# Attention scores of two maps: from zero-padded queries on all 128 rows of the array to the two halves of 64 rows

## The reference, cut to what matters

```python
logits = jnp.einsum('bqhmd,bkhmd->bhmqk', q, k).astype(jnp.float32) * (DA_DH ** -0.5)   # m: the two maps, d: 64
logits = jnp.where((dist >= 0)[None, None, None], logits + bias[None, :, None], -1e30)
p = jax.nn.softmax(logits, axis=-1)
attn = p[:, :, 0] - lam * p[:, :, 1]
return jnp.einsum('bhqk,bkhv->bqhv', attn, v.astype(jnp.float32))
```

## Time and profile before

| | |
|---|---|
| median of 3 runs | 1911.32 us (1902.96 to 1913.05) |
| the profiled execution's own time | 1919.13 us |
| its span, first to last instruction | 1917.2 us |
| PE busy over the span | 1675.8 us (87%) |
| DVE, ACT, POOL busy | 714.6, 454.0, 255.2 us |
| mean granted PE clock, share of full | 0.932 |
| the attention phase on PE | from 486 us (bias) or 491 us (first z) to 911.5 us |

### The profile page before, as it was taken

How to read it: one execution, slowest core, us unless ns; L and a number is a source line. 1 busy time by engine, 2 the same in 40 slices (tenths; PEclk the granted TensorE clock), 3 DMA queues, 4 the chain that set the end, 5 groups by cost and what they waited for, 6 DMA issues and landing times. The chain is left out here.

```text
span 1917.2 us, 22028 instructions
## 1 busy us (share of the span) xinstructions
PE 1675.8 (87%) x7437; PEld 1114.3 (58%) x7438; DVE 714.6 (37%) x1501; ACT 454.0 (24%) x1062; POOL 255.2 (13%) x447
## 2 busy tenths in 40 slices
PE   5998889975898989897789699999989946999996
PEld 4565555655455655565344588888867833444443
DVE  4367676676244444534122321111132241222111
ACT  2233333232243333333121311011032210111110
POOL 1000101010221222221313000000000001222221
PEclk8999899987898989998899799999989967999998
DMA  7001200000302020000866211121043364988873
GB/s 219 1 1 56 67 1 24 1 24 2 95 1 57 1 58 0 25 1 24 272 214 217 80 34 34 34 65 34 1 125 103 124 208 144 303 246 238 244 214 62
DMA packets 135895, 175.00 MB, mean 91 GB/s; under 512 B 9523, under 2 KB 106854, under 8 KB 135798
## 3 DMA queue, kind: packets, MB, share of 16 engines
q1 hardware_dynamic: 123190, 129.71, 21.4%
q0 software_dynamic: 12608, 44.05, 8.5%
HBM read 142.86 MB, written 30.87 MB: 91 GB/s over the span
## 5 line engine op out<-in xcount | busy, mean ns | idle before, releaser
L941 PE MATMUL psum<-branch_part,kept 128*128 128x384 f32 (+1 forms) x576 | 205.6, 514 | 1.2 <-DVE branch_part L1171 1.2
L2164 PE MATMUL psum<-moe_part,kept 128*128 x416 | 185.6, 599 | 5.9 <-issue 4.3
L941 PEld LDWEIGHTS psum<-branch_part,kept 128*128 128x128 f32 (+1 forms) x576 | 110.7, 197 | 78.6 <-issue 22.2
L475 PE MATMUL psum<-kept,branch_part 128*128 128x368 f32 x384 | 125.2, 482 | 10.0 <-PEq L218 5.0
L1598 PE MATMUL psum<-kept,merge_part 128*128 128x368 f32 x384 | 125.2, 480 | 9.5 <-DMA merge_part<-w_da_out 9.5
L1604 PE MATMUL psum<-split 128*128 128x368 f32 x384 | 133.4, 347 | 0.0
L2164 PEld LDWEIGHTS psum<-moe_part,kept 128*128 128x128 f32 x416 | 77.6, 192 | 95.4 <-issue 94.8
L480 PE MATMUL psum<-branch_part,kept 128*128 128x512 f32 (+1 forms) x288 | 127.6, 598 | 1.3 <-DVE kept L661 1.3
L1605 PE MATMUL psum<-split 128*128 128x368 f32 x384 | 126.9, 330 | 0.0
L1606 PE MATMUL psum<-split 128*128 128x368 f32 x384 | 126.5, 329 | 0.0
L1653 DVE TENSOR_TENSOR merge_part<-merge_part,psum 128x368 f32<-128x368 f32 x48 | 23.6, 534 | 253.6 <-ACT merge_part L1629 253.6
(11 more groups left out here) (321 smaller groups left out, 2701.9 us busy)
## 6 DMA issues: line engine op xcount, KB each, us to landing
branch_part<-cache_k SPq DMA_DIRECT2D x64, 256.0 KB, 4.8
branch_part<-cache_v POOLq DMA_DIRECT2D x64, 256.0 KB, 5.1
moe_part<-w_gate SPq DMA_DIRECT2D x16, 1024.0 KB, 7.0
moe_part<-w_up SPq DMA_DIRECT2D x16, 1024.0 KB, 13.2
moe_part<-w_down SPq DMA_DIRECT2D x16, 1024.0 KB, 14.0
branch_part<-w_in SPq DMA_DIRECT2D x8, 1024.0 KB, 8.8
merge_part<-w_in SPq DMA_DIRECT2D x16, 512.0 KB
branch_part<-w_in SPq DMA_DIRECT2D x12, 512.0 KB
```

The lines of the kernel that those rows point to most:

```text
L475: mm = pe.matmul(bank[:, 0:CH], Wb[0][:, k, c0:c0 + P], K["xT"][:, k, CH * i:CH * i + CH], start=(k == 0), stop=(k == KC - 1))
L941: mm = pe.matmul(bank_of(("z", h, i))[:ROWS[i], 0:384], K["xT"][:, k, cols(i)], Wb[h % 2][:, k, :], start=(k == 0), stop=(k == KC - 1))
L2164: mm = pe.matmul(psum[:, 2 + par, :], XT[par][:, k, :], K["GU"][:, bass.ds(KC * b + k, 1), :], start=(k == 0), stop=(k == KC - 1))
```

## The change

The two zero-padded copies `qz` become one `qT` of the same 128 rows without zeros. Scores of map 0 are a matmul on rows 0 to 63 of query and key, scores of map 1 one on rows 64 to 127. The jobs L(s,0) and L(s,1) become one job, in which each piece (up to 512 columns) is issued for map 0 and then for map 1. `place_qk` copies the queries in one instruction instead of two. The two memsets go. `save` copies each half of the rows for itself, with a drain of POOL ahead of each copy and one more. In `meta_scores` PE waits, between the maps, for its own first matmul.

```diff
-            slot += [("L", s, 0), ("L", s, 1)] + ([("e", s, 0)] if s % NQ == NQ - 1 else [])
+            slot += [("L", s, 0)] + ([("e", s, 0)] if s % NQ == NQ - 1 else [])
...
-        qz = [sb(2, TOK) for _ in range(2)]
+        qT = [sb(TOK) for _ in range(2)]
...
-            def scores(s, m):
+            def scores(s):
                 h, i = s // NQ, s % NQ
                 r = P if i else META
-                q = qz[h % 2][:, m, COL[i]:COL[i] + r]
-                if m == 0:
-                    pe.wait_ge(x_done, NT * h + i + 1)
-                    if s:
-                        pe.wait_ge(exp_done, 2 * s)
+                rows = [slice(64 * m, 64 * m + 64) for m in range(2)]
+                pe.wait_ge(x_done, NT * h + i + 1)
+                if s:
+                    pe.wait_ge(exp_done, 2 * s)
                 n = P * i
-                for c in range(0, n, 512):
-                    w = min(512, n - c)
-                    mm = pe.matmul(lg[m][:r, c:c + w], q, kT[h % 2][:, FIRST + c:FIRST + c + w], start=True, stop=True)
-                if n < SEQ:
-                    mm = pe.matmul(lg[m][:r, n:n + META], q, kT[h % 2][:, 0:META], start=True, stop=True)
-                    mm.then_inc(logits, 1)
-                elif m == 0:
-                    mm.then_inc(logits, 1)
+                pieces = [(c, min(512, n - c), FIRST + c) for c in range(0, n, 512)] + [(n, META, 0)] * (n < SEQ)
+                for at, w, key in pieces:
+                    for m in range(2):
+                        mm = pe.matmul(lg[m][:r, at:at + w], qT[h % 2][rows[m], COL[i]:COL[i] + r], kT[h % 2][rows[m], key:key + w], start=True, stop=True)
+                        if at + w >= n and (n == SEQ or at == n) and (n < SEQ or m == 0):
+                            mm.then_inc(logits, 1)
...
+                    if m == 0:
+                        mm.then_inc(meta_scored, 1)
+                        pe.wait_ge(meta_scored, h + 1)
                 mm.then_inc(logits, 1)
...
-                for m in range(2):
-                    rows = slice(64 * m, 64 * m + 64)
-                    act.activation(qz[h % 2][rows, m, cols(i)], bank[rows, 0:r], ACT.Copy, scale=K["vecT"][rows, 18:19])
+                act.activation(qT[h % 2][:, cols(i)], bank[:, 0:r], ACT.Copy, scale=K["vecT"][:, 18:19])
...
-            for h in range(2):
-                pool.memset(qz[h].rearrange("p a b -> p (a b)"), 0.0).then_inc(setup, 1)
             pool.memset(K["Qs"].rearrange("p a b -> p (a b)"), 0.0).then_inc(setup, 1)
-            pool.wait_ge(setup, 3)
+            pool.wait_ge(setup, 1)
```

More of the change, by code:

```diff
@@ L852, in phase_attention @@
         kv_out = [sem("kv_out0"), sem("kv_out1")]
+        meta_scored = sem("meta_scored")
         Wb = [sb(KC, 384) for _ in range(2)]
-        qz = [sb(2, TOK) for _ in range(2)]
+        qT = [sb(TOK) for _ in range(2)]
         kT = [sb(TOK) for _ in range(2)]
@@ L974, in meta_scores @@
                 for m in range(2):
-                    mm = pe.matmul(bank_of(("e", s, 0))[:, META * m:META * m + META], qz[h % 2][:, m, cols(i)],
-                                   kT[h % 2][:, 0:META], start=True, stop=True)
+                    rows = slice(64 * m, 64 * m + 64)
+                    mm = pe.matmul(bank_of(("e", s, 0))[:, META * m:META * m + META], qT[h % 2][rows, cols(i)],
+                                   kT[h % 2][rows, 0:META], start=True, stop=True)
+                    if m == 0:
+                        mm.then_inc(meta_scored, 1)
+                        pe.wait_ge(meta_scored, h + 1)
                 mm.then_inc(logits, 1)
@@ L1013, in _ @@
                 pe.matmul(psum[:, h, 0:ND], relh[0:33, h, :], bucket[0:33], start=True, stop=True).then_inc(bias_made, 1)
-            run = {"z": product, "x": turn_qk, "L": scores, "e": lambda s, _: meta_scores(s), "a": turn_probabilities,
+            run = {"z": product, "x": turn_qk, "L": lambda s, _: scores(s), "e": lambda s, _: meta_scores(s), "a": turn_probabilities,
                    "o": lambda s, _: outputs(s), "g": lambda s, _: turn_output(s)}
@@ L1042, in place_qk @@
                 act.wait_ge(x_turned, n + 1)
-                if n == 0:
-                    act.wait_ge(setup, 3)
                 if i == 0 and h >= 2:
                     act.wait_ge(saved, h - 1)
-                for m in range(2):
-                    rows = slice(64 * m, 64 * m + 64)
-                    act.activation(qz[h % 2][rows, m, cols(i)], bank[rows, 0:r], ACT.Copy, scale=K["vecT"][rows, 18:19])
+                act.activation(qT[h % 2][:, cols(i)], bank[:, 0:r], ACT.Copy, scale=K["vecT"][:, 18:19])
                 act.activation(kT[h % 2][:, cols(i)], bank[:, P:P + r], ACT.Copy).then_inc(x_done, 1)
@@ L1138, in save @@
                 for m in range(2):
-                    pool.tensor_copy(K["Qs"][:, DB * h:DB * h + DB, 16 * h + 8 * m:16 * h + 8 * m + 8],
-                                     qz[h % 2][:, m, META:FIRST].rearrange("p (b s) -> p b s", s=DS))
+                    rows = slice(64 * m, 64 * m + 64)
+                    pool.drain()
+                    pool.tensor_copy(K["Qs"][rows, DB * h:DB * h + DB, 16 * h + 8 * m:16 * h + 8 * m + 8],
+                                     qT[h % 2][rows, META:FIRST].rearrange("p (b s) -> p b s", s=DS))
+                pool.drain()
                 pool.tensor_copy(K["kS"][:, h, :], kT[h % 2][:, 0:FIRST]).then_inc(saved, 1)
```

## The result

The changed kernel takes 1930.22 us (median of 4 runs, 1927.18 to 1933.03). The kernel before, run beside it, takes 1909.61 us (1902.96 to 1913.05). The ratio is 1.0112, 95% interval 1.0079 to 1.0145. So the change costs about 21 us, or 1.1%. 1920 was forecast, with a range of 1905 to 1940.

What follows compares the result with a forecast made beforehand. The prediction took each attention slot to be bound by map 0's scores and DVE up to `normalise`, not by PE. Its terms, -2.0 + 3.8 - 2.0 + 8.7 = +8.5 us, gave 1920 us against 1911.32, range 1905 to 1940.

Steps and rivals of the forecast that it cites:

- The chain of the slot: Attention slot: it ends when DVE has normalised; from map 0's end to x are 4.01 us, map 1's 1.73 beside them.
- Entering the halves, +3.8: Scores in blocks 4 to 8: switching PE to 64-row halves delays map 0 by 0.19 us in 20 slots, +3.8 us.
- map 1 no longer in DVE's way, -2.0: Scores: DVE no longer waits for map 1, which ends beside map 0; 0.5 us a head, -2.0 us.
- The start, -2.0: Start of attention phase: with two memsets gone DVE's copy is quicker and bias matmuls start 2.7 us earlier; -2.0 us taken.
- The clock, +8.7: Slots of blocks 4 to 7: longer PE waits drop the clock in 5 of 16 slots, 1.73 us each, +8.7 us.
- slower: Whole kernel: time more than 0.5%, some 9.6 us, above the kernel before; chance 0.46.
- within: Whole kernel: time within 0.5%, some 9.6 us, of the kernel before, told as no change; chance 0.45.
- Rival A: PE's clock in the attention phase: waits of 1 to 2 us leave it alone, sum -0.2 us, 1911 us; chance 0.15.
- B: Scores on PE: the halves do not run together, so DVE starts later; +34.5 us, 1946 us; chance 0.17.
- C: Attention phase: PE is the bound after all, so the 31 us saved on scores come out; 1878 us; chance 0.08.

Runs made afterwards that it cites:

- the second one: Trace of the kernel before, run again with no edit, against the kernel before: 1909.69 us, ratio 1.0009.
- the last experiment: Changed kernel with `normalise` ahead of the maxima, plus four useless 512-column matmuls ahead of the outputs in each slot of block 8, against the kernel before: 1886.11 us, ratio 0.9877.

## Why the prediction was right, and where it was not

- *The chain of the slot* (map 0, DVE's maxima of both maps, `normalise`, x): right. PE's scores shrank by 31 us, only the slot of block 8 became shorter by it (0.35 us), and the wait for `normalise` grew from 27.7 to 50.5 us; "about 60" was forecast. Interleaving the padded maps lengthened the slots by way of this chain. With `normalise` first the halves do pay, as the chain says, though the time came out 24 and 37 us above what I expected of it.
- *Entering the halves, +3.8, and map 1 no longer in DVE's way, -2.0*: together about nothing. At full clock the slots of block 3 differ by less than 0.2 us either way, those of blocks 4 and 5 are 0.14 us longer, that of 6 0.07, that of 7 unchanged, and that of 8 some 0.35 shorter: about 0 a head, where +0.45 was forecast. The start of DVE in block 7 came 0.10 us later, not 0.19; the pause between the maps is gone, as said.
- *The start, -2.0*: -1.3 against the trace that it was read from, and +0.2 to +0.5 against the second one, where the copy took 1.77 us. The copy is as quick as hoped for (0.42 us; 0.8 was worked out); the weights of z, whose landing I could not see, then cost 1.77 us.
- *The clock, +8.7*: the term that was mis-sized. The runs give 17 to 24.5 us. Against the very trace that I read, it is right: 7.7 us, and the traced run of the changed kernel took 1927.18 us where 1927.6 was worked out. But that execution of the kernel before had more falls than usual (seven z of 7 us, the other trace two). I took its 7.8 us above the median for a constant and moved the sum down by it; the changed kernel has its ten z of 7 us in both traces, so its usual run doesn't move down with it. I priced a fall well (z 7.0 us instead of 5.3). I looked only at slots of blocks 4 to 7: falls came in blocks 2, 3 and 8 too. I had worked out that the wait in block 8 grows to some 4.5 us (it is 4.0) and charged it nothing, though the last experiment shows, with `normalise` first, that idle time there is dear. And I took idle time as the only cause: with the wait between the maps PE is busier than before, and the clock is at 0.925 all the same.
- The error of +10 us against the forecast is thus the clock's. By the table the clock gives up to +24.5 instead of +8.7, and the other terms -3.5 instead of -0.2: +21.0 where +8.5 was added up. That 1930 still lies in the range owes something to the range's width: by my price of 1.73 us a fall, 24.5 us are 14 falls of the 16 that I thought possible.
- *The chances*: by the prediction's own line of 0.5% the result is "slower", which had 0.46, against 0.45 for "within". So it was right on the mechanism and the range, but it did not call the sign with any confidence.
- *Rival A* (the clock holds) is refuted by the clock of every run of the changed kernel (0.922 to 0.928, against 0.936 on average before), *B* by the pair of matmuls that starts at once, *C* (PE is the bound) by the waits of PE, which grew as its work shrank; with `normalise` first it comes nearly true.

What is still open: whether rows that a matmul leaves unused lower the clock as such, or only the pauses around them; and why some slots lose the clock in one execution and keep it in the next.

## What to carry to other kernels

Read which engine ends a slot before an edit speeds up another one: halving work beside the chain gave nothing here at full clock. Idle time that it leaves on TensorE wasn't free, since the next product, which is on the chain, could run at half the clock; so put the order right first, and then ask what fills the longest idle time. Filler helped only where PE stood idle anyway, and here the longest idle stretch was worth more than many short ones. Compare the mean clock of many runs, not one profile.

## What the runs showed of the hardware

- Two float32 matmuls on different halves of the rows start together (both 693 ns, within 30 ns). Twelve MATMUL instructions, six for each map, take 1.83 us from start to start, where the six of one map on full rows took 1.64.
- A matmul on the free half can start ahead of earlier ones queued for the other: with map 0's pieces issued first, the scores of block 8 take 1.99 us as when interleaved, the first of each map 0.01 us apart. With six instructions ahead (block 7) it starts 0.97 us later. With a wait between the maps they take 3.85 us in block 7, where the two orders take 1.90 and 2.86.
- The granted clock fell after 6.90 us in which PE was shown busy for 6.76, 2.13 of them on half the rows.
- DVE's copy of 33x512 takes 0.42 us alone, and 1.77 or 3.52 us beside POOL's memsets. By the Trainium skill (SBUF — State Buffer, SBUF: two separate sides) the two share a port pair, which one of them locks for a whole instruction. The runs agree that the copy is held up.
- The same 8 float32 matmuls of z take 5.3 to 5.4 us at 2.4 GHz, and 7.0 us where the clock went to 1.2 GHz at their start.
